# Down projections of two feed-forward blocks by seven block products over even and odd tiles

## What is computed

```python
def swiglu(h, w_gate, w_up, w_down):
    return (jax.nn.silu(h @ w_gate) * (h @ w_up)) @ w_down

x = x + 0.5 * swiglu(rms_norm(x, ffn1_norm), ffn1_w_gate, ffn1_w_up, ffn1_w_down)
...
x = x + 0.5 * swiglu(rms_norm(x, ffn2_norm), ffn2_w_gate, ffn2_w_up, ffn2_w_down)
return rms_norm(x, final_norm)
```

## Time and profile before

| | |
|---|---|
| median of 3 runs | 2666.89 us (2664.64 to 2670.21) |
| the profiled execution | 2670.37 us |
| its span | 2668.4 us |
| TensorE busy | 2560.3 us, 96% of the span |
| weight loads of TensorE | 2057.3 us, 77% |
| VectorE, ScalarE, GpSimd busy | 1482.2, 1071.6, 1035.5 us |

### The profile page before, as it was taken

How to read it: one execution, slowest core, us unless ns; L and a number is a source line. 1 busy time by engine, 2 the same in 40 slices (tenths; PEclk the granted TensorE clock), 3 DMA queues, 4 the chain that set the end, 5 groups by cost and what they waited for, 6 DMA issues and landing times.

```text
span 2668.4 us, 32264 instructions
## 1 busy us (share of the span) xinstructions
PE 2560.3 (96%) x12859; PEld 2057.3 (77%) x12859; DVE 1482.2 (56%) x1829; ACT 1071.6 (40%) x1702; POOL 1035.5 (39%) x700
## 2 busy tenths in 40 slices
PE   8999998988979999999999999899999999999998
PEld 6778775668868788888787887666687888887876
DVE  7665576766575864445224447677559445432334
ACT  5443445643444433333324333666444333333332
POOL 2212122575015565555332344311347455543232
PEclk9999998999989999999999999999999999999999
DMA  4222415352135121222444332100341222225343
GB/s 156 84 90 103 149 40 223 102 181 73 53 115 178 60 105 72 91 81 89 172 171 142 127 123 86 61 9 1 106 139 56 87 95 75 77 100 212 133 154 111
DMA packets 113813, 285.73 MB, mean 107 GB/s; under 512 B 27704, under 2 KB 27896, under 8 KB 113536
## 3 DMA queue, kind: packets, MB, share of 16 engines
q1 hardware_dynamic: 113664, 283.68, 30.1%
HBM read 221.70 MB, written 61.93 MB: 106 GB/s over the span
## 4 chain that ended last, share of the span: by engine, by line
PE 81%; DVE 9%; POOL 4%; ACT 4%; issue 2%; DMA 1%; SPq 0%; DVEq 0%; ACTq 0%; POOLq 0%
PE ps L347 22%; PE ps L349 22%; PE ps L348 22%; PE ps L897 2%; PE ps L913 2%; PE ps L933 2%; ACT t L363 2%; PE ps L531 1%; POOL t L1384 1%; POOL t L1381 1%; ACT t L996 1%; PE ps L1491 1%; DVE t L1047 1%; POOL t L2540 1%; PE ps L1499 1%
## 5 line engine op out<-in xcount | busy, mean ns | idle before, releaser
L363 ACT ACTIVATE t<-t 128x512 fp32r<-128x512 f32 (+5 forms) x1015 | 718.0, 743 | 1238.4 <-PE ps L349 839.6
L347 PE MATMUL ps<-t 128*128 128x512 f32 x2874 | 1132.8, 394 | 23.2 <-DVE t L571 10.5
L348 PE MATMUL ps<-t 128*128 128x512 f32 x2874 | 1118.0, 389 | 0.0
L349 PE MATMUL ps<-t 128*128 128x512 f32 x2874 | 1117.8, 389 | 0.0
L347 PEld LDWEIGHTS ps<-t 128*128 128x128 f32 x2874 | 541.6, 188 | 144.7 <-issue 25.0
L348 PEld LDWEIGHTS ps<-t 128*128 128x128 f32 x2874 | 541.7, 188 | 116.5 <-issue 6.7
L349 PEld LDWEIGHTS ps<-t 128*128 128x128 f32 x2874 | 541.4, 188 | 112.2
L2540 POOL TENSOR_TENSOR t<-t 128x512 fp32r<-128x512 f32 x280 | 411.4, 1474 | 367.8 <-ACT t L363 367.8
L447 POOL TENSOR_TENSOR t<-t 128x1024 fp32r<-128x1024 f32 x86 | 214.2, 2495 | 546.2 <-ACT t L363 546.2
L2324 DVE TENSOR_TENSOR t<-ps,t 128x512 f32<-128x512 f32 x200 | 137.3, 688 | 291.8 <-PE ps L349 291.6
L452 DVE TENSOR_TENSOR t<-t 128x1024 fp32r<-128x1024 f32 x96 | 125.8, 1310 | 291.8 <-ACT t L363 291.8
(11 more groups left out here) (184 smaller groups left out, 2188.5 us busy)
## 6 DMA issues: line engine op xcount, KB each, us to landing
t<-in_wts_dram SPq DMA_DIRECT2D x262, 512.0 KB, 3.5
g_d<-t SPq DMA_DIRECT2D x84, 256.0 KB, 2.2
t<-g_d SPq DMA_DIRECT2D x84, 256.0 KB, 3.3
t<-pj SPq DMA_DIRECT2D x39, 512.0 KB, 5.6
pj<-t SPq DMA_DIRECT2D x32, 512.0 KB, 2.7
x_d<-t SPq DMA_DIRECT2D x32, 256.0 KB, 4.2
t<-x_d SPq DMA_DIRECT2D x32, 256.0 KB, 5.7
t<-in_rpb_dram SPq DMA_DIRECT2D x8, 736.0 KB, 7.8
```

Source lines behind the costliest of these rows:

```text
L347: e.matmul(out, ah, bh, start=start, stop=False, skip_group_check=goes_on)
L348: e.matmul(out, ah, bl, start=False, stop=False, skip_group_check=goes_on)
L349: return e.matmul(out, al, bh, start=False, stop=stop, skip_group_check=goes_on)
L363: return e.activation(out, in_, fn, scale=scale)
```

## The change

The sum over inner tiles 0 to 19 is taken as a product of 2 x 2 blocks: the weights' blocks are (outputs 0 to 3 or 4 to 7) by (even or odd inner tiles), those of gate x up are (even or odd inner tiles) by (half of the tokens). Seven products P1 to P7 take the place of eight. With the tiles in pairs, each product has ten items (one pair k each) of four output tiles, 12 matmuls an item; inner tiles 20 and 21 are added in the plain way ("more") for each of the four result blocks. An item is one left block of 128 x 512 (four weight tiles) and one right block of 128 x 512. There are 78 items instead of 44 steps of up to 24 matmuls.

- Left: weight blocks of 256 KB are loaded into buffers that the last gate x up unit frees (`slots`, `LOADS`; A11, A21 and A22 during that unit, A12 and A22 again during the stage). VectorE forms S1 to S4 (`dve_left_sum`, 40 a feed-forward part) and the small part of every left block (`dve_item`). ScalarE casts the large one.
- Right: in gate x up, VectorE forms T1 to T4 of each unit's quarters (`dve_right_sums`, 4 a unit), and 7 blocks a unit go to DRAM instead of 4. In the down stage each item's block is loaded (`sp_item`), cast by ScalarE, and its small part is made by GpSimd (`pool_item`).
- Results: a product's accumulator is added to every block of `x` that it belongs to (`dve_out`); three pairs of products go on in the same banks. The items run P1, P6, P2, P7, P5, c22 ("more" alone), P3, P4; the last four of P4 are run output by output.
- `x` comes back three tiles an item, from item 5 on. `pe_factor` runs behind the sixth item of P4. The weights of the next stage are loaded and cast near the end, not step by step.

```diff
-DOWN = [FT - 2, FT - 1] + list(range(FT - 2))
...
+DOWN_PRODUCTS = (("P1", "A11", "B11", None), ("P6", "S2", "T2", None), ("P2", "A12", "B21", (0, 1)), ("P7", "S3", "T3", None),
+                 ("P5", "S1", "T1", None), ("c22", None, None, (1, 0)), ("P3", "S4", "B22", (0, 0)), ("P4", "A22", "T4", (1, 1)))
+ITEMS = []
+for _name, _left, _right, _more in DOWN_PRODUCTS:
+    if _left:
+        ITEMS += [(_name, _left, _right, _k) for _k in range(UNITS)]
+    if _more:
+        ITEMS += [(_name, "more", _more, _x) for _x in range(2)]
+NI = len(ITEMS)
+FIRST = {p[0]: min(i for i in range(NI) if ITEMS[i][0] == p[0]) for p in DOWN_PRODUCTS}
+LAST = {p[0]: max(i for i in range(NI) if ITEMS[i][0] == p[0]) for p in DOWN_PRODUCTS}
+PLACES = NI // 2
+EXTRA = 3 * UNITS + PLACES
+GOES_ON = {"P2": "P1", "P7": "P6", "P3": "P5"}
+SUMS_IN = {"P1": "a1", "P2": "a1", "P6": "b1", "P7": "b1", "P5": "a2", "P3": "a2", "c22": "b2", "P4": "b3"}
...
+            early = (self.pieces(range(4), 0) + self.pieces(range(4, KC), 0) + self.sum_pieces(2) + self.sum_pieces(0))
+            self.slots = {"A11": early[0:10], "A21": early[10:20], "A22": early[20:30],
+                          "N": early[30:32] + self.pieces(range(4), 1),
+                          "A12": self.pieces(range(4, KC), 1) + [self.F.t[:, 1, :], self.F.t[:, 2, :]]}
+            self.early = [(n, k) for n in ("A11", "A21", "A22") for k in range(UNITS)]
...
+        def down(i, m):
+
+            prod, left, _, k = ITEMS[i]
+            key, first, last, on = (P.name, SUMS_IN[prod], m), i == FIRST[prod], i == LAST[prod], prod in GOES_ON
+            if first and on:
+                w.wait_ge(f_ev, (P.name, GOES_ON[prod], m))
+            elif first:
+                until = {"a1": P.x_ready(1, m), "b1": (f_ev, (P.name, "P7", m)), "a2": P.x_ready(0, m),
+                         "b2": P.x_ready(0, 4 + m), "b3": P.x_ready(1, 4 + m)}[key[1]]
+                if prod == "P4":
+                    for sg, at in banks.share(key, (P.name, "b2", m), [until])[1]:
+                        w.wait_ge(sg, at)
+                else:
+                    pe_slot(w, key, [until], banks)
+            first = first and not on
+            p, a = banks[key], tok[m]
+            (hi, lo), (_, gh, gl) = P.left(i), P.entry(i)
+            if left == "more" and k:
+                e.matmul(p, hi[:, a], gh, start=first, stop=False, skip_group_check=on)
+                return e.matmul(p, lo[0:64, a], gh[0:64, :], start=False, stop=last, skip_group_check=on)
+            return mm3(e, p, (hi[:, a], lo[:, a]), (gh, gl), first, last, on)
...
+        for i in range(NI - 4):
+            ready(i)
+            for m in range(4):
+                at = down(i, m)
+            at.then_inc(*d_used.up((P.name, i)))
+            if i == LAST["P3"] + 5:
+                pe_factor(e, w, P.after, 0)
+        for i in range(NI - 4, NI):
+            ready(i)
+        for m in range(4):
+            for i in range(NI - 4, NI):
+                at = down(i, m)
+                if m == 3:
+                    at.then_inc(*d_used.up((P.name, i)))
+            if m < 3:
+                at.then_inc(*b_dn.up((P.name, m)))
...
+    def dve_item(e, w, P, i):
+
+        hi, lo = P.left(i)
+        w.wait_ge(d_hi, (P.name, i))
+        e.tensor_tensor(lo, P.left_source(i)[0], hi.bitcast(F), SUB).then_inc(*d_lo.up((P.name, i)))
+        raw, gh, _ = P.entry(i)
+        if halved(i):
+            w.wait_ge(f_gh, (P.name, i))
+            e.tensor_tensor(gh[64:128, :], raw[0:64, :], gh[0:64, :].bitcast(F), SUB).then_inc(*f_gl_v.up((P.name, i)))
+
+    halved = lambda i: ITEMS[i][1] == "more" and ITEMS[i][3] == 1
+    right_done = lambda P, i: (f_gl_v if halved(i) else f_gl, (P.name, i))
...
+    def pool_item(e, w, P, i):
+
+        if not halved(i):
+            raw, gh, gl = P.entry(i)
             w.wait_ge(f_gh, (P.name, i))
             e.tensor_tensor(gl, raw, gh.bitcast(F), SUB).then_inc(*f_gl.up((P.name, i)))
...
+    def dve_left_sum(e, w, P, what, k):
+
+        if not 0 <= k < UNITS:
+            return
+        a11, a12, a21, a22, n = (P.slots[x][k] for x in ("A11", "A12", "A21", "A22", "N"))
+        if what == "S1":
+            loaded(w, P, "A21", k)
+            loaded(w, P, "A22", k)
+            m = e.tensor_tensor(a22, a21, a22, ADD)
+        elif what == "S2":
+            loaded(w, P, "A11", k)
+            w.wait_ge(f_s, (P.name, "S1", k))
+            w.wait_ge(s_used, (P.name, 14 * (UNITS - 1) + (9 if k < 2 else 11)))
+            m = e.tensor_tensor(n, a22, a11, SUB)
+        elif what == "S3":
+            w.wait_ge(f_s, (P.name, "S1", k))
+            m = e.tensor_tensor(a21, a11, a21, SUB)
+        else:
+            loaded(w, P, "A12", k)
+            w.wait_ge(d_lo, (P.name, FIRST["P6"] + k))
+            m = e.tensor_tensor(n, a12, n, SUB)
+        m.then_inc(*f_s.up((P.name, what, k)))
...
+    def dve_right_sums(e, w, P, p):
+
+        g11, g12, g21, g22 = (P.g(p, i) for i in range(4))
+        t1, t2, t4 = (P.sum_slot(i) for i in range(3))
+        w.wait_ge(f_g, (P.name, p, "12"))
+        if p:
+            w.wait_ge(g_out[(p - 1) % 2], (P.name, p - 1, "T4"))
+        e.tensor_tensor(t1, g11, g12, SUB).then_inc(*f_tb.up((P.name, p, "T1")))
+        w.wait_ge(f_tb, (P.name, p, "T1"))
+        e.tensor_tensor(g11, g21, g11, SUB).then_inc(*f_tb.up((P.name, p, "T3")))
+        e.tensor_tensor(t2, g21, t1, SUB).then_inc(*f_tb.up((P.name, p, "T2")))
+        w.wait_ge(f_tb, (P.name, p, "T2"))
+        e.tensor_tensor(t4, g22, t2, SUB).then_inc(*f_tb.up((P.name, p, "T4")))
...
+                at = e.scalar_tensor_tensor(x, banks[P.name, SUMS_IN[prod], m], 0.5, x, MUL, ADD)
...
         for p in range(UNITS):
             if p:
+                dve_sums(e, w, P, p, 1, ("S3", "S4"))
                 gated(p - 1, "12")
-                dve_sums(e, w, P, p, 1, ("S3", "S4"))
+                dve_right_sums(e, w, P, p - 1)
...
+        for i in range(NI):
+            dve_left_sum(e, w, P, "S1", i + 4)
+            dve_left_sum(e, w, P, "S2", i - 5)
+            dve_left_sum(e, w, P, "S3", i - 22)
+            dve_left_sum(e, w, P, "S4", i - 36)
+            if i + 3 < NI:
+                dve_item(e, w, P, i + 3)
+            at = i - FIRST["P6"]
+            if 0 <= at < 8:
+                out("P1", at // 2, (0, 1) if at % 2 == 0 else (2,))
+            at = i - FIRST["P2"]
+            if 0 <= at < 4:
+                out("P6", at)
+            at = i - FIRST["P7"]
+            if 0 <= at < 4:
+                out("P2", at)
+            if 1 <= at < 5:
+                squared(1, at - 1)
+            at = i - FIRST["P5"]
...
+            if at == 6:
+                dve_factor(e, w, P.after, 0)
+            if 7 <= at < 11:
+                if P.after == "mixn":
+                    dve_operand(e, w, "mixn", 0, at - 7, P.T)
+                else:
+                    dve_result(e, w, 0, 2 * (at - 7))
+                    dve_result(e, w, 0, 2 * (at - 7) + 1)
+        for m in range(4):
+            out("P4", m)
+            if m:
+                squared(1, 3 + m)
...
+    def act_item(e, w, P, i):
+        src, ready = P.left_source(i)
+        w.wait_ge(*ready)
+        place_free(w, P.item_place + i // 2, i % 2)
+        act(e, P.left(i)[0], src, ACT.Copy).then_inc(*d_hi.up((P.name, i)))
         raw, gh, _ = P.entry(i)
-        r = rows_at(DOWN[i % FT])
+        r = slice(0, 64 if ITEMS[i][1] == "more" and ITEMS[i][3] else 128)
         w.wait_ge(g_in[i % 4], (P.name, i))
-        w.wait_ge(*((w_used, P.down[i - 4]) if i >= 4 else (s_used, (P.name, 14 * (UNITS - 1) + 3))))
+        w.wait_ge(*((d_used, (P.name, i - 4)) if i >= 4 else (s_used, (P.name, 14 * (UNITS - 1) + 3))))
         act(e, gh[r, :], raw[r, :], ACT.Copy).then_inc(*f_gh.up((P.name, i)))
 
...
+    def sp_item(e, w, P, i):
+
+        if i >= NI:
+            return
+        _, left, what, k = ITEMS[i]
+        w.wait_ge(*(right_done(P, i - 4) if i >= 4 else (s_lo, (P.name, 14 * (UNITS - 1) + 12))))
+        r = slice(0, 128)
+        if left == "more":
+            w.wait_ge(g_out_c[k], (P.name, 2 * UNITS + k, 1))
+            r, src = slice(0, 64 if k else 128), more_at(k, what[1])
+        else:
+            w.wait_ge(g_out[k % 2], (P.name, k, "T4"))
+            src = right_at(what, k)
+        e.dma_start(P.entry(i)[0][r, :], src[r, :]).then_inc(*g_in[i % 4].up((P.name, i)))
...
+        for x in LOADS[0:8]:
+            sp_left(e, w, P, *x)
+        late(UNITS - 2)
+        for x in LOADS[8:24]:
+            sp_left(e, w, P, *x)
+        for i in range(4):
+            sp_item(e, w, P, i)
+        for x in LOADS[24:30]:
+            sp_left(e, w, P, *x)
+        out(UNITS - 1, "22")
+        out(UNITS - 1, "21")
+        late(UNITS - 1)
+        rows = [(row, s) for s in (0, 1) for row in range(KC)]
+        for i in range(4, NI):
+            sp_item(e, w, P, i)
```

(26 more changed lines are left out.)

380 lines of the change are left out of this document (181 added, 199 removed).

## The result

| | before | after | after / before, 95% interval |
|---|---|---|---|
| first comparison, median | 2666.97 us | 2624.79 us | 0.9839 [0.9822, 0.9856] |
| with the first experiments | 2670.42 us | 2628.11 us | 0.9844 [0.9831, 0.9858] |
| with the last experiments | 2667.16 us | 2624.80 us | 0.9840 [0.9826, 0.9853] |
| profiled execution, own time / span | 2670.4 / 2668.4 us | 2625.6 / 2623.5 us | |

A forecast was written before the change was run, and what follows sets the result against it. TensorE was taken as the bound, busy 2560.3 of 2668.4 us. -54.4 (fewer matmuls) + 2 x (1.2 start + 2.0 end - 1.0 middle) = -50.0 us: 2620.4 against the profiled 2670.4, forecast 2617 against the median 2666.9, range 2610 to 2621.

The forecast's parts named there:

- crowded start: Rival: at the down stage's start right loads land in 7.2 us and wait behind x; 2622 to 2629, chance 0.14.
- The gain: Down stages: 120 matmuls fewer a part at an unchanged pace of 0.2267 us, 54.4 us saved for both parts.
- Gate x up: Four VectorE subtractions at each unit's turn and seven writes a unit instead of four cost nothing.
- The middle: Down stage at `pe_factor`: the 1.3 us wait for squares mostly goes, -1.0 us a part.
- The end: Before the output-by-output end, item 77's right buffer gives no lead, so TensorE waits: +2.0 us a part.
- The start: Down stage's start: item 4's load stands behind the last unit's writes, the last being T4; +1.2 us a part.
- Nothing waits: Rival: item 4's load lands at once and the item-77 wait hides; -57, 2610 us, chance 0.06.
- VectorE and GpSimd become the bound: Rival: down-stage items with a sum take 4.27 us, 112 us more, 2729; chance 0.03, mild form (2638) 0.03.

The follow-up runs named there:

- end3: Changed kernel with the output-by-output end over the last three items instead of four; 2619.14 us, ratio 0.9813 to the kernel before.
- s1late: Changed kernel with the four S1 sums of items 0 to 3 moved from the last gate x up unit into the items; 2626.51 us, ratio 0.9840.
- rightdve: Changed kernel with the right blocks' small part made by VectorE too, GpSimd doing nothing in the items; 2623.14 us, ratio 0.9823.
- again: The changed kernel run once more with no edit; 2628.11 us, ratio 0.9844 to the kernel before.
- early47: Changed kernel with the loads of items 4 to 7 issued ahead of the last unit's last five writes; 2635.44 us, ratio 0.9867.
- comb2: Changed kernel with three end items, early loads of items 4 to 7, late S1 sums, VectorE's item 3 step behind item 2's; 2622.51 us, ratio 0.9821.
- best: Changed kernel with both small parts of an item on VectorE and the output-by-output end over three items; 2613.91 us, ratio 0.9802.
- leftpool: Changed kernel with the left blocks' small part made by GpSimd instead of VectorE; 2662.09 us, ratio 0.9970.
- end3b: Second run of the changed kernel with the output-by-output end over three items instead of four; 2622.08 us, ratio 0.9826.
- comb: Changed kernel with both three items at the end and the early loads of items 4 to 7; 2625.42 us, ratio 0.9835.
- again2: The changed kernel unedited, third time; 2624.80 us, ratio 0.9840 to the kernel before.

## Why the prediction was right, and by how much it was off

**The range.** The mechanism was right in the main; that the number fell inside the stated range is in part luck. I had given 0.72 to 2610 to 2621, and 2624.8 lies above it, in the 2622 to 2629 of the crowded start, which happened only in small. The range of the terms was also added up wrongly: the ends that I state for them give -54.4 + 2 x (0 + 1.6 - 1.3) = -53.8 to -54.4 + 2 x (2.0 + 2.7 - 0) = -45.0, that is 2613 to 2622, which the measured time still exceeds by 3 us.

**The gain** was right: 240 matmuls fewer, and over 30 us with 29.85 us of VectorE no gap. **Gate x up** was right too: the four subtractions at a unit's turn and three more writes cost nothing. **The middle** was right: -1.2 us against -1.0; the matmul behind the wait of 1.3 us now starts 0.46 us after the one ahead of it.

**The end** was right in its mechanism, as end3 shows, and too small. I had 2.0 us a part; the spacing of the matmuls there exceeds the pace by 2.2 us in the first part and 2.9 in the second, in all three traces of the changed kernel. That is 1.1 us more in both together.

**The start** is the step that failed in its working, though its size is near: 1.2 us a part were predicted, and 1.6 are the mean of six starts (2.2 and 1.0, 1.8 and 1.8, 1.7 and 1.3). The step said that T1 to T4 follow the last multiplication and "end near 1302.3". They ended at 1305.70 in a stage that began 1.0 us later, so 2.4 us late. And item 3's wait of 0.70 us for VectorE's own step, and item 6's behind the tiles of `x`, were not in the step at all. The reason for the first two stands in the prediction itself, under what works beside TensorE: operations with both inputs in SBUF go one after another. I costed that at nothing because the small parts run three items ahead. At the start there is no such lead, and VectorE's list holds what SyncE waits for. A quicker landing paid part of it back: 2.8 us for item 4, where I had reckoned with 2.6 to 4.4. All loads of right blocks after the change:

```profile
DMA to landing us min/median/max: 2.3/2.7/7.8
```

s1late and rightdve bear both halves out: with four sums less in the list T4 ends 1.6 us earlier, with GpSimd silent 1.9.

**Left out of the sum.** Some 0.6 us a part are in the stages and in none of my terms (23.2 + 24.0 measured, 24.0 + 24.5 with the waits as measured). In the first stage about 0.35 of it are the second matmuls behind the four waits, spaced 0.31 to 0.34 us instead of 0.23, and 0.16 the start of item 7. The changes between whole and 64-row tiles add nothing: the first spacing there is 0.32 instead of 0.43, the one behind the group 0.33 instead of 0.23, before the change as after.

These corrections, 2 x 0.4 at the start, 1.1 at the end, -0.4 in the middle and 1.2 here, are 2.7 us, and lead from -50.0 to the -47.2 of the first trace within 0.1. From there to the -42.3 of the medians three things count. In the mean of the three traces of the changed kernel the two parts fell by 45.2 us and not 47.2, which is the **clock**: I had taken it as 1.00 throughout, and it was so in the down stages of before and in the first trace after, but in the two later ones 10.2 and 3.4 us of them went at 1.2 GHz, half of it lost, 2.3 us in the mean of three. The stages outside were 0.5 us longer in that mean. And the one profiled execution of before, at 2670.4 us, lies 2.2 us above its medians, which flatters the change. That leaves 0.2 us. How much of the clock's other stretches, outside these stages, belongs to the change can't be said from one trace of before.

**The rivals.** The crowded start happened in small: item 6, whose load stands behind three tiles of x and took 5.5 us to land, came 0.25 us late in the first trace, and 0.7 in the second stage of again, against the 5.7 us a part of that rival; item 10, the first that needs x, did not wait. It was crowded where I moved nine tiles of x up myself (item 8 in early47 and comb2). "Nothing waits" is what best shows: 2613.9, against 2610. "VectorE and GpSimd become the bound" did not happen, but leftpool shows how near it was: one more subtraction an item on GpSimd takes 36 of the 42 us. One number of the prediction bears on this: VectorE's additions to x are 44 a stage after the change, 28 more than before, and not 28 as written there; TensorE missed nothing by it. The price in leftpool doesn't come from a full list all along, as I had argued it: the middle of the stage and half of the start's wait come from one engine being shut out by the other, and about a third of the price is clock behind the waits; only the end is a list that is late. The Trainium skill, "SBUF — State Buffer", section "Who interferes with whom", says that the second of two such engines is fully blocked while the port is held; the 0.55 us behind GpSimd's end and the 0.68 us of rightdve agree. As a sum of durations the rule gave the 2.65 us an item that I used; what counted in leftpool was who gets the port next.

## What to carry to other kernels

When work is split between VectorE and GpSimd and both inputs of VectorE's operations lie in SBUF, it is not parallel: ask what stands behind the held operation in its list. Here the same subtractions all on VectorE cost less than the split (best against end3b measured beside it, 2613.9 against 2622.1 us), and two an item on GpSimd nearly ended the gain. And before a stretch that wants several items at once, count the buffers: the last item's must come free a step before the stretch begins.

## What the runs showed of the hardware that I had not expected

GpSimd can shut VectorE out: 22.59 us for an operation of 0.68, with GpSimd's starts 1.25 us apart. It goes both ways: at the start of leftpool's first down stage six sums of VectorE in a row kept a step of GpSimd at 4.36 us. But in the run of four at the start of the changed kernel's stage VectorE got its turn after one step (1.78 us), and so it did in leftpool itself: its T1 to T4 took 1.7 us each between four steps of GpSimd 1.70 us apart, though ScalarE's casts for these had all ended by 1294.00, at least 1.4 us ahead. So inputs that lie ready don't decide alone who is shut out; what does stays open.

A wait of TensorE can cost more than its length. At each wait of 3.6 us or more in a down stage (early47, comb, six in leftpool) the granted clock fell to 0.50 near its end and stayed there for 3.4 to 13.7 us. At the end waits of 1.8 to 2.7 us it fell in some executions and not in others (again and s1late both, again2 the first, after neither). It also fell without a wait, in the traces of comb, end3, end3b, rightdve (twice) and best, each time during or directly behind eight matmuls that alternate between whole and 64-row tiles, 0.43 us apart; as here in best, where the first window holds seven of these eight:

```profile
2523.00:2526.50 3.50, 3.50 (x10) 1.58 (x9) 2.98 (x5) 1.29 (x3) 0.00 (x0) 1.00 0.25 70
2526.50:2530.00 3.50, 3.50 (x10) 2.73 (x9) 1.89 (x3) 1.01 (x2) 0.00 (x0) 0.51 0.52 143
```

There are six such groups in every trace, and most pass without it. What decides in a given execution stays open.
